# Expert rows gathered in pairs: dot and weighted sum slot by slot, with a 128x128 diagonal per slot

## The reference, cut to what matters

```python
q = (xb @ wq).reshape(TOKEN_BLOCK, PEER_HEADS, 2, PEER_DQ // 2)      # 8 heads, 2 x 128
s = jnp.einsum('thcd,ckd->thck', q, subkeys)                          # 128 keys on each side
sv, si = lax.top_k(s, PEER_TOPK)                                      # best 16 of each side
cand = sv[:, :, 0, :, None] + sv[:, :, 1, None, :]                    # 256 sums
top_v, top_pos = lax.top_k(cand, PEER_TOPK)                           # best 16 sums
eidx = ...                                                            # si0 * 128 + si1
g = jax.nn.softmax(top_v, axis=-1)
a = jax.nn.gelu(jnp.einsum('td,thkd->thk', xb, u_tab[eidx]))          # 128 dots of 1024 per token
out = jnp.einsum('thk,thkd->td', g * a, v_tab[eidx])                  # 128 weighted rows per token
```

## Time and profile before

| | |
|---|---|
| median of 3 runs | 4904.78 us (4903.73 to 4910.56) |
| the profiled execution | 4917.18 us, of which span 4915.5 us |
| PE, DVE, ACT, POOL busy | 78%, 60%, 9%, 46% of the span |
| gathers (queue q0) | 1124.21 MB, 61.2% of the time of 16 DMA engines |
| chain of waits | POOL 23%, DMA 17%, PE 12% |

### The profile page before, as it was taken

The page is one execution under the profiler, slowest core; times in us unless marked ns, Lnnn a source line. Parts: engine busy times, 40 slices in busy tenths (PEclk is TensorE's granted clock), DMA queues, the critical chain, the costliest instruction groups (busy, mean ns, idle before and its releaser), DMA issues.

```text
span 4915.5 us, 38276 instructions
## 1 busy us (share of the span) xinstructions
PE 3810.6 (78%) x11459; PEld 1541.3 (31%) x11459; DVE 2952.9 (60%) x7681; ACT 437.3 (9%) x1045; POOL 2278.9 (46%) x2121
## 2 busy tenths in 40 slices
PE   5699899899999853157777777767777777777789
PEld 3355355355445432112222222222222222211122
DVE  4466656646656658866666666656666656666620
ACT  2112112112212200000000000000000000000000
POOL 0000000000000014567767767767767767777765
PEclk7799999999989976589999999999989999999999
DMA  4210410410410146789999999999999999999999
GB/s 149 56 44 19 125 38 25 124 37 20 129 37 19 44 173 205 244 299 372 383 350 380 386 340 380 379 340 384 378 347 386 374 344 374 375 365 376 377 351 344
DMA packets 387569, 1213.27 MB, mean 247 GB/s; under 512 B 60792, under 2 KB 101296, under 8 KB 386392
## 3 DMA queue, kind: packets, MB, share of 16 engines
q0 software_dynamic: 308112, 1124.21, 61.2%
q1 hardware_dynamic: 79304, 87.29, 5.7%
HBM read 1181.66 MB, written 29.14 MB: 246 GB/s over the span
## 4 chain that ended last, share of the span: by engine, by line
POOL 23%; DMA 17%; PE 12%; issue 8%; DVE 6%; ACT 0%; SPq 0%; DVEq 0%; ACTq 0%; POOLq 0%
DMA weights<-in_peer_v,c_idxT 13%; POOL weights L1588 12%; POOL c_ub L1588 11%; PE c_acc L1710 7%; DMA c_ub<-in_peer_u,c_idx 3%; PE c_po L1636 2%; DVE c_ub L1902 2%; PE c_pq L1659 1%; DMA weights<-mixT_d 1%; PE c_acc L1700 1%; DVE c_hot L1855 0%; DVE c_hot L1851 0%; DVE c_es L1857 0%; DVE c_yt L1879 0%; PE c_po L1719 0%
## 5 line engine op out<-in xcount | busy, mean ns | idle before, releaser
L1710 PE MATMUL c_acc<-weights,c_Z 128*32 128x512 f32 x4096 | 1721.0, 602 | 532.8 <-DMA weights<-in_peer_v,c_idxT 530.5
L1902 DVE CUSTOM_DVE_ANT_0 c_ub<-c_ub,c_h 128x1024 f32<-128x1024 f32 x1024 | 1242.6, 1224 | 936.0 <-DMA c_ub<-in_peer_u,c_idx 930.5
L1588 POOL DMA_INDIRECT weights<-in_peer_v,c_idxT x1024 | 1148.8, 1122 | 413.1 <-issue 213.6
L1588 POOL DMA_INDIRECT c_ub<-in_peer_u,c_idx x1024 | 1068.6, 1044 | 509.1 <-issue 295.7
L821 PE MATMUL b_pj<-weights,b_hcB 128*128 128x512 f32 (+1 forms) x2560 | 1025.4, 558 | 1.1 <-ACT b_s_v L1049 1.1
L1710 PEld LDWEIGHTS c_acc<-weights,c_Z 128*32 128x32 f32 x4096 | 346.4, 109 | 1777.8 <-DMA weights<-in_peer_v,c_idxT 1136.7
L821 PEld LDWEIGHTS b_pj<-weights,b_hcB 128*128 128x128 f32 x2560 | 488.5, 192 | 489.1 <-issue 474.4
L482 POOL DMA_DIRECT2D weights<-in_w_in x40 | 36.0, 911 | 1113.9 <-PE b_pj L821 1091.8
L1659 PE MATMUL c_pq<-c_wq,weights 128*128 128x256 f32 (+1 forms) x1152 | 276.8, 395 | 2.3 <-ACT weights L1735 2.3
L1659 PEld LDWEIGHTS c_pq<-c_wq,weights 128*128 128x128 f32 (+1 forms) x1152 | 209.0, 186 | 81.4 <-issue 41.8
L1742 ACT ACTIVATE c_qs<-c_pq 128x256 f32<-128x256 f32 (+1 forms) x72 | 27.5, 382 | 1981.0 <-PE c_pq L1659 1981.0
(11 more groups left out here) (340 smaller groups left out, 3085.0 us busy)
## 6 DMA issues: line engine op xcount, KB each, us to landing
weights<-in_w_in POOLq DMA_DIRECT2D x32, 1024.0 KB, 8.1
b_hcB<-hT_d SPq DMA_DIRECT2D x32, 512.0 KB, 3.6
c_ub<-in_peer_u,c_idx POOLq DMA_INDIRECT x1024, 6.1
weights<-in_peer_v,c_idxT POOLq DMA_INDIRECT x1024, 6.2
b_s_C<-in_state_mlstm_c SPq DMA_DIRECT2D x8, 1024.0 KB, 12.7
out_s_c<-b_s_C SPq DMA_DIRECT2D x8, 1024.0 KB
c_wq<-in_peer_wq SPq DMA_DIRECT2D x4, 2048.0 KB, 18.7
a_x<-in_x_prompt SPq DMA_DIRECT2D x8, 512.0 KB, 4.5
```

The costliest lines, as they stand in the source:

```text
L1588: nc.gpsimd.indirect_dma_start(out=out, out_offset=None, in_=io[table], in_offset=bass.IndirectOffsetOnAxis(ap=at, axis=0)).then_inc(loade ...
L1710: last = nc.tensor.matmul(acc[half][j * SUB:(j + 1) * SUB, :], Z[:, lo:lo + SUB], vb[:, turn % RV, half * 512:(half + 1) * 512], start=Fal ...
L1902: nc.vector.tensor_tensor_reduce(ub[:, turn % RU, :], ub[:, turn % RU, :], h2[:, b, :], 1.0, 0.0, ALU.mult, ALU.add, a[:, b, k:k + 1]).the ...
```

## The change

`u` and `v` become one step per slot. POOL gathers the slot's row of `peer_u` and its row of `peer_v` for the 128 tokens with the same indices, one after the other, into the two halves of one of RB = 7 buffers of 8 KB per partition. DVE forms the dots from the first half. ACT takes the one column of dots through Gelu, multiplies it by the softmax share, and scales the identity by it: a 128x128 diagonal, in one of RD = 4 buffers. PE multiplies the diagonal with the second half of the buffer and adds to `acc`, which now exists twice (for tiles n and n+1). The buffer is free for POOL when PE is done with it. `Z`, `fill`, `idxT`, `wT` and the separate `v` gathers go; the number of gathers and of bytes stays.

The order: after head 0 of tile 0 the slots begin at once. The other seven heads of tile 0 follow in slots 1 to 49, seven slots each, one search step per slot; the work for tile n+1 stands in tile n's slots: `out` at slots 8 and 9 with `norm2` at 9, `hT` at 11, `start` at 13, and head h at slots 12+14h to 18+14h (for n = 0: from slot 50, heads 9 slots apart; for n = 7, the sample: from slot 3, 10 apart). `softmax` is done per head, as a seventh search step. `squares` and `final` of tile n-1 stand at slot 4 of tile n. There is only one `psc`, and `q` uses the two banks of `po`.

```diff
-RU = 4
-RV = 6
-V_LAG = 4
+RB = 7
+RD = 4
...
+    def head(n, hd):
+        return [(what, n, hd) for what in ("q", "qT", "sc", "best", "sums", "pick", "softmax")]
...
+        def put(at, items):
+            for step, item in enumerate(items):
+                extra.setdefault(at + step, []).append(item)
+
+        if n == 0:
+            for hd in range(1, PH):
+                put(1 + 7 * (hd - 1), head(0, hd))
+        first, each = (50, 9) if n == 0 else (8, 14) if n + 1 < CHUNKS else (3, 10)
+        m = n + 1
+        put(first, [("out", m, 0)])
+        put(first + 1, [("out", m, 1), ("norm2", m, 0)])
+        put(first + 3, [("hT", m, 0)])
+        if n:
+            put(4, [("squares", n - 1, 0), ("final", n - 1, 0)])
+        put(first + 5, [("start", m, 0)])
+        for hd in range(PH):
+            put(first + 4 + each * hd, head(m, hd))
...
         for o in range(SLOTS):
             order += extra.get(o, [])
...
+            order.append(("u", n, o))
...
+                after(pool, row_used, turn - RB + 1)
+                for table, half in (("peer_u", 0), ("peer_v", D)):
+                    nc.gpsimd.indirect_dma_start(out=rows_b[turn % RB][:, half:half + D], out_offset=None, in_=io[table],
+                                                 in_offset=bass.IndirectOffsetOnAxis(ap=at, axis=0))\
+                        .then_inc(row_loaded[turn % RB], 16)
...
+                elif what in ("u", "us"):
+                    turn, final = turns[n, k], k == (SLOTS if what == "u" else PH) - 1
+                    pe.wait_ge(diag_done, turn + 1)
                     for half in range(2):
...
+                        last = nc.tensor.matmul(acc[b][half][0:rows, :], diag[:, turn % RD, 0:rows],
+                                                rows_b[turn % RB][:, D + half * 512:D + (half + 1) * 512],
+                                                start=False, stop=final)
+                    last.then_inc(row_used, 1)
...
+                    act.wait_ge(dot_done, turn + 1)
+                    nc.scalar.activation(gelu, dot, ACT.Gelu).then_inc(gelu_done, 1)
+                    if what == "u" and k % TOPK == 0:
+                        act.wait_ge(g_done, n * PH + k // TOPK + 1)
+                    act.wait_ge(gelu_done, turn + 1)
+                    nc.scalar.activation(weight, gelu, ACT.Copy, scale=share).then_inc(w_done, 1)
+                    act.wait_ge(w_done, turn + 1)
+                    after(act, row_used, turn - RD + 1)
+                    nc.scalar.activation(spread, ones, ACT.Copy, scale=weight).then_inc(diag_done, 1)
...
                     turn = turns[n, k]
+                    dve.wait_ge(row_loaded[turn % RB], 32 * (turn // RB) + 32)
+                    nc.vector.tensor_tensor_reduce(rows_b[turn % RB][:, 0:D], rows_b[turn % RB][:, 0:D], h2[:, b, :],
+                                                   1.0, 0.0, ALU.mult, ALU.add, a[:, b, k:k + 1]).then_inc(dot_done, 1)
```

More of the change, by code:

```diff
@@ L1341, in peer_schedule @@
 def peer_schedule():
[L1343 to L1355, removed]
-        extra = {}
[L1357 to L1365, removed]
-            for h in range(PH):
[L1367 to L1372, removed]
+    def head(n, hd):
+        return [(what, n, hd) for what in ("q", "qT", "sc", "best", "sums", "pick", "softmax")]
@@ new lines, in peer_schedule @@
+    order = [("out", 0, 0), ("out", 0, 1), ("keysT", 0, 0), ("norm2", 0, 0), ("hT", 0, 0), ("start", 0, 0)]
+    order += head(0, 0)
+    for n in range(CHUNKS):
+        extra = {}
+        def put(at, items):
[14 more added lines that the diff above has]
+            put(first + 4 + each * hd, head(m, hd))
+        if m == CHUNKS:
+            for h in range(PH):
+                put(108 + 2 * h, [("us", m, h)])
+            put(126, [("squares", m, 0), ("final", m, 0)])
@@ L1383, in peer_schedule @@
[L1383 to L1390, removed]
+            order.append(("u", n, o))
+    order += [("squares", CHUNKS - 1, 0), ("final", CHUNKS - 1, 0)]
+    return order
 def peer(nc, io, res):
@@ L1468, in peer @@
         consts_done = sem("consts_done")
-        zeros_done = sem("zeros_done")
         sub_done = sem("sub_done")
@@ L1748, in _ @@
                 elif what == "softmax":
-                    act.wait_ge(idx_done, n * PH + PH)
-                    nc.scalar.activation(tvm[0:rows], tvm[0:rows], ACT.Exp).then_inc(exp_done, 1)
-                elif what == "gelu":
-                    act.wait_ge(u_used, u_turn[n, SLOTS - 1] + 1)
-                    after(act, w_done, n)
-                    nc.scalar.activation(ga[:], a[:, b, :], ACT.Gelu).then_inc(gelu_done, 1)
-                elif what == "fill":
-                    act.wait_ge(wT_done, n + 1)
-                    if n:
-                        act.wait_ge(v_used, v_turn[n - 1, SLOTS - 1] + 1)
-                    nc.scalar.activation(
-                        Z[:, 0:SLOTS * SUB].rearrange("p (s j c) -> p j s c", j=NSUB, c=SUB)[:, :, :, SUB - 1],
-                        pT[:, 2 * P:3 * P].rearrange("p (j s) -> p j s", j=NSUB), ACT.Copy).then_inc(fill_done, 1)
+                    act.wait_ge(idx_done, hh + 1)
@@ new lines, in _ @@
+                    nc.scalar.activation(tvm[0:rows, k], tvm[0:rows, k], ACT.Exp).then_inc(exp_done, 1)
+                elif what in ("u", "us"):
+                    turn = turns[n, k]
+                    if what == "u":
+                        dot, gelu, weight = a[:, b, k:k + 1], ga[:, b, k:k + 1], w[:, b, k:k + 1]
+                        share, spread, ones = g[:, b, k:k + 1], diag[:, turn % RD, :], ident[:]
+                    else:
+                        dot, gelu, weight = a_r[:, k:k + 1], ga_r[:, k:k + 1], w_r[:, k:k + 1]
+                        share, spread, ones = g_r[:, k:k + 1], diag[:, turn % RD, 0:NS], sel[:]
+                    act.wait_ge(dot_done, turn + 1)
[7 more added lines that the diff above has]
+                    nc.scalar.activation(spread, ones, ACT.Copy, scale=weight).then_inc(diag_done, 1)
@@ L1771, in _ @@
                     last.then_inc(squares_done, 1)
-                elif what == "gelu_s":
-                    heads = slice(k * PH // 2, (k + 1) * PH // 2)
-                    act.wait_ge(u_used, u_turn[n, (k + 1) * PH // 2 - 1] + 1)
-                    nc.scalar.activation(a_r[:, heads], a_r[:, heads], ACT.Gelu).then_inc(gelu_s_done, 1)
         @block.vector
```

219 lines of the change are left out of this document (64 added, 155 removed).

## The result

The changed kernel takes 5351.99 us (median of 4 runs, 5336.44 to 5360.02) against 4906.48 us (4903.73 to 4910.56) for the kernel before on the same chip: a ratio of 1.090, 95% interval 1.088 to 1.093. The forecast was 5260 us; the time lies 92 us (1.7%) above it and inside the range. The profiled execution has a span of 5349.2 us, where the sum gave 5272.

A forecast was written before the change was run, and what follows sets the result against it. POOL's gather issue, 2.73 us a pair, was taken as the bound. First gather 1781.3, tile 0 557, tiles 1 to 6 2465, tile 7 460 and end 8.6 sum to 5272 us span; as a median 5260 us, range 4960 to 5540.

The forecast's parts named there:

- Part 1: The u-only and v-only stretches become one more tile of pairs: 192 us saved at the floor, gone in tile 0.
- Part 2: Each slot's way from POOL's issue to buffer free takes 11.7 us; seven buffers hide a delay of 7.1 us.
- Part 3: After a stall PE needs 1.72 us a slot, so consumers recover 1.0 us per slot instead of 2.1.
- Part 4: A head's seven search slots take 30.0 us; 42.0 per 14 slots against 38.2, so a head costs 3.8 us.
- part 6: PE's granted clock falls behind idle time: 3 us a tile, and 2 us on each of tile 0's 15 heads.
- Part 5: A tile's first 15 slots take 79.7 us against 41.0; less the ring's 7.1, 31.6 us are lost.
- Tile 7: The last tile, with eight heads of 10 slots at 282 us, was to take 460 us together.
- Shorter chains: Rival: hand-overs overlap and a head's search slots take 27 us; 5057 us, as a median 5045; chance 0.20.
- Half clock in the searches: Rival: PE at half clock in each of 71 heads' searches adds 284 us, 5545 us; chance 0.13.
- Faster: Rival: the ring of buffers hides all delays of heads and tile starts; 4617 us, 4605 as a median; chance 0.08.
- Later landings: Rival: a slot's gathers land after 9.3 us instead of 6.3, some 160 us more, 5420 us; no separate chance.
- The drain: Rival: ACT's table loads carry a drain of 1.38 us, 71 times, 98 us on top, 5360 us; chance 0.04.

The follow-up runs named there:

- lagged2: The changed kernel with only its list reordered: search steps two slots apart, ACT's copies and DVE's softmax later, tile starts drawn apart; 4684.53 us, 0.952 of before.
- soft_later: The changed kernel with DVE's part of each head's softmax two slots after ACT's Exp; 5296.81 us, 1.078 of the kernel before.

## Why the prediction was right, and where its sizes were off

The mechanism and the sign were right. Span 5349.2 against the 5272 of the sum, +77.3: first gather 1789.4 (+8.1), tile 0 536 (-21), tiles 1 to 6 2537 (+72.4), tile 7 and end 486.4 (+17.8). The last 15 us of the 92 are that the median was taken 12 us below the profiled execution, as before; this time it lies 1 us above. The 8.1 us of the first gather are within the scatter of the mixer (see above). What the prediction named as signs came: two table loads a head of 1.28 us, POOL waiting for PE, 14 pairs in 44.1 us (42), a tile of 423 us (411), tile 0 of 536 (550).

- *Part 1, fill and drain*: 192 us were put down and called lost in tile 0. Tile 0 does take 186 us more than 128p here. That the gain is there to be had, `lagged2` shows: from the first gather to the last matmul into `acc` it takes 2883 us (1781.4 to 4664.5), where before 3124 stood (1783.1 to 4906.9), 241 less. Of these some 109 are seven tiles of 353.1 us for 368.7; the other 132 are fill and drain.
- *Part 2, the chain of a slot*: the hand-over from dot to PE is longer than 0.78 us. ACT's three operations are 0.20, 0.29 and 0.40 us (page: 200, 294, 401 ns), where 0.20, 0.20 and 0.30 stood. The first was right by its row; the second is an ACT operation with a column as its scale, and the third was taken from the 128x128 Exp, which has none. With the gaps it is 0.95 us (2904.46 to 2905.41), near the upper bound that was given. The landing was 5.9 and 6.1 us by the page's median, for 6.3.
- *Part 3, catching up*: 12.9 us for seven slots, 1.84 each, for 12.0. On PE the chain's eight slots take 15.70 us: two of them 5.24, most of it at 1.2 GHz behind PE's idle time, the others 1.74 each, as the sum had it (1.72).
- *Part 4, the head*: 31.2 us against 30.0, and 44.1 against 42.0 with the seven between. By step: `q` 7.4 (6.6), `qT` 3.75 (3.7; 4.0 with the head whose slot has `start`), `sc` and `best` together 7.65 (7.4), `sums` 3.99 (4.0), `pick` 3.97 (4.0), softmax 4.33 (4.3). The steps that DVE sets were exact. In the `q` slot 16 records, 1.33 us of PE's idle time and four records make 3.62 + 1.33 + 1.98 = 6.9 of it; the rest is that PE still has earlier slots to work off when the last diagonal is there. A head costs 44.1 - 38.2 = 5.9 us instead of 3.8. This term makes +14.5 us a tile, less the 3 us of part 6 nearly the whole miss of the tiles. The larger part of it is the clock, which the sum had left out here: the two slots behind softmax take PE 4.7 us from start to start on average over 42 heads (3.5 to 5.2), where 2 x 1.72 = 3.4 stood, 1.3 of the 2.1 us. ACT's hand-over, 0.95 for 0.78, makes part of the rest.
- *Part 5, the tile's start*: 80.5 us against 79.7, so 80.5 - 41.0 - 7.1 = 32.4 lost instead of 31.6. Two slots were read off by one: `put` sets each item of its list one slot on, so that `norm2` stands at slot 10 and `final` at slot 5, not at 9 and 4. Slots 4 to 11 take 47.5 us for 48.0, so the slip cost nothing: `norm2` waits for the same half of `out`. Slots 12 to 18 take 33.0 for 31.7. The parts add up to the tile: 349.7 + 32.4 + 7 x 5.9 = 423.4; measured 421.2 to 425.4.
- *Part 6, the clock*: this term was put in the wrong places. The 3 us a tile are within the 80.5 of the start; the heads of tiles 1 to 6 had nothing, and pay the 1.3 us each of part 4, 9 us a tile. In tile 0 30 us were put down, 2 us on each of 15 heads. By its parts tile 0 took 8.7 (fill, 9.5), 218.0 (seven heads, 210), 34.0 (slots 50 to 53, 35.0), 271.9 (eight heads with `start`, 268.7) and 3.5 us (3.4): 9.4 us more than the sum without the clock, so at most a third of the 30 was there (PEclk 0.89, for 0.90 and 0.92 in the tiles). That these 20 us too many stand against what the heads lack is luck; without them the forecast would lie 112 us off and not 92. The four records behind `best` take 3.66 us after 3.51 us of idle time (0.43 us a record at full clock), but they aren't on the path: PE is idle again for 0.37 us before the next diagonal. The clock was not tried alone.
- *Tile 7*: 474 for 460, all of the 14 us in its eight heads (296 us for 282). Eight of its gathers, one a head, take over 2.4 us, up to 7.52; see below. What they cost was not tried.

The rivals. *Shorter chains* (B) is false: the head is 31.2 us, not 27. (Its tile 0 of 492 us doesn't follow from its terms, 557 - 15 x 3 = 512, so its price was 5077 us of span and not 5057.) *Half clock in the searches* (D) is a part, not the case: 1.3 us a head on the path, in the slots behind softmax, where D had 4.0 in `q` and the transposes; and PEclk in the tiles is 0.90 and 0.92. *Faster* (C) is false for this order: the seven slots take 31.2 us and not under 26.2, the first fifteen 80.5 and not under 48. With another order its state is nearly reached: in `lagged2` POOL waits 83 us in all for PE's buffers, 5.4 at most, and the time is 4685 us, against 4605 for C. *Later landings* are false too: 5.9 and 6.1 us, not 9.3. *The drain* (E) is false: the load begins 0.02 us behind the diagonal (2924.42 + 0.40 to 2924.84), the Exp 0.01 us behind the load. The Trainium skill, "ScalarE: Activation LUTs", What ACT_TABLE_LOAD costs, puts the drain of about 1.38 us on top; the trace has none beside 1.28 us. What the two loads of a head do cost is `soft_later`'s: a slot of 3.80 us.

## What to carry to other kernels

When one list sets the order of all engines and a slot's work passes from engine to engine, the cost of a side job is what it holds of the chain, less what the ring of buffers covers: 31.2 + 12.9 us against 14 x 2.73. Work that is put one piece per slot into adjacent slots adds its holds up faster than the ring can absorb them; with a slot free between two pieces, and each piece's hand-over one slot later than its making, the same instructions cost next to nothing (667 us here, 12.5%). So before fusing a producer's and a consumer's step into one slot, sum the holds over as many slots as the ring is deep, and draw up the order first.
